# One Trainium2 core, mixer, cross-attention and routed experts: six PSUM banks and reordered evictions in the front, another order of the last eight weight chunks

## The reference

```python
hn = rmsnorm(h, g_mix); proj = hn @ w_in                  # 2048 columns: u | B | C | v
y_pool = pool_mixer(u, w_pool, pool_scale)                # trailing means over 2, 4, 8, 16 frames, 4 linear maps
y_conv = B * causal_conv3(C * v)
h = h + concat(y_pool, y_conv) @ w_out
h = h + mem_cross_attention(rmsnorm(h, g_xattn), rmsnorm(mem, g_mem), w_q, w_k, w_v, w_o)   # 4 heads of 256
xt = rmsnorm(h, g_moe); top 4 of 32 experts by xt @ w_router + b_router, gates = softmax(top 4)
gu = xt[tok] @ w_gate_up[e] + b_gate_up[e]                # 1024 -> 2048
act = (clip(gu_up, -7, 7) + 1) * (min(gu_gate, 7) * sigmoid(1.702 * min(gu_gate, 7)))
h[tok] += gate * (act @ w_down[e] + b_down[e])
out = rmsnorm(h, g_final)
```

## Time and profile before

| | |
|---|---|
| median of 3 runs | 1146.5 us (1143.35 to 1148.73) |
| profiled execution | 1145.61 us, its span 1143.9 us |
| front, to the last matmul of the logits | about 216 us |
| first chunk of the experts used | about 231 us |
| experts, 402.7 MB of weights | the rest |
| HBM read | 435.47 MB |
| granted TensorE clock, mean | 0.992 |

### The profile page before, as it was taken

How to read it: one execution, slowest core, us unless ns; L and a number is a source line. 1 busy time by engine, 2 the same in 40 slices (tenths; PEclk the granted TensorE clock), 3 DMA queues, 4 the chain that set the end, 5 groups by cost and what they waited for, 6 DMA issues and landing times.

```text
span 1143.9 us, 12842 instructions
## 1 busy us (share of the span) xinstructions
PE 1076.5 (94%) x5419; PEld 489.2 (43%) x5420; DVE 342.6 (30%) x573; ACT 197.7 (17%) x323; POOL 26.1 (2%) x53
## 2 busy tenths in 40 slices
PE   8979999999999999999999999999999989999995
PEld 7978997733333333333333333333332333333332
DVE  8555645312222222222222222222222212222223
ACT  6523544400000000000000110100000000000002
POOL 6200000000000000000000000000000000000000
PEclk9999999899999999999999999999999999999998
DMA  9964555789999999999999999999999999999993
GB/s 351 349 212 146 170 221 229 286 365 428 427 426 427 430 427 427 427 429 427 427 426 429 428 428 426 429 427 428 427 429 426 428 427 428 429 427 426 429 429 156
DMA packets 52007, 437.94 MB, mean 383 GB/s; under 512 B 5184, under 2 KB 23024, under 8 KB 27376
## 3 DMA queue, kind: packets, MB, share of 16 engines
q1 hardware_dynamic: 51856, 437.10, 92.0%
q10 hardware_dynamic: 96, 0.02, 0.0%
HBM read 435.47 MB, written 1.05 MB: 382 GB/s over the span
## 4 chain that ended last, share of the span: by engine, by line
PE 63%; DMA 25%; DVE 8%; ACT 2%; issue 1%; ACTq 0%; DVEq 0%
PE ps L734 26%; DMA slot<-in_w_gate_up 25%; PE ps L768 14%; PE ps L476 7%; PE ps L534 6%; PE ps L779 3%; PE ps L752 2%; DVE glu L1338 2%; DVE lin L1335 2%; DVE glu L1331 2%; DVE lin L1332 1%; ACT sig L824 1%; PE ps L499 1%; PE ps L723 1%; ACT w_hi L824 1%
## 5 line engine op out<-in xcount | busy, mean ns | idle before, releaser
L734 PE MATMUL ps<-slot,xT 128*64 128x512 f32 x2048 | 456.9, 595 | 17.2 <-DMA slot<-in_w_gate_up 16.4
L734 PEld LDWEIGHTS ps<-slot,xT 128*64 128x64 f32 x2048 | 142.0, 136 | 310.4 <-issue 266.1
L768 PE MATMUL ps<-slot,sig 128*64 128x512 f32 x1024 | 226.8, 595 | 8.0 <-ACT sig L824 8.0
L1344 DVE TENSOR_TENSOR h_rows<-ps,h_rows 128x1024 f32<-128x1024 f32 x64 | 75.4, 1219 | 368.3 <-PE ps L779 368.3
L768 PEld LDWEIGHTS ps<-slot,sig 128*64 128x64 f32 x1024 | 70.7, 137 | 143.6 <-issue 127.9
L995 ACT ACTIVATE sig<-glu 128x512 f32<-128x512 f32 x32 | 20.2, 632 | 546.3 <-DVE glu L1331 546.3
L1331 DVE TENSOR_SCALAR glu<-ps 128x512 f32<-128x512 f32 x32 | 22.1, 692 | 280.1 <-PE ps L734 280.1
L1093 DVE TENSOR_TENSOR w_lo<-ring,w_hi 128x1024 fp32r<-128x1024 f32 x56 | 68.2, 1225 | 74.7 <-ACT w_hi L824 74.6
L824 ACT ACTIVATE xg_sb<-ps 128x512 f32<-128x512 f32 x65 | 38.9, 598 | 245.3 <-PE ps L768 230.0
L824 ACT ACTIVATE w_hi<-ring 128x1024 fp32r<-128x1024 f32 x56 | 59.0, 1062 | 83.8 <-PE ps L476 52.3
L779 PE MATMUL ps<-xg_sb,g_sb 64*128 64x512 f32 x256 | 63.6, 615 | 0.7 <-ACT xg_sb L824 0.7
(11 more groups left out here) (190 smaller groups left out, 708.8 us busy)
## 6 DMA issues: line engine op xcount, KB each, us to landing
slot<-in_w_gate_up SPq DMA_DIRECT2D x128, 2048.0 KB, 36.4
slot<-in_w_down SPq DMA_DIRECT2D x64, 2048.0 KB, 37.5
ring<-in_w_in SPq DMA_DIRECT2D x8, 1024.0 KB, 13.9
ring<-in_w_v SPq DMA_DIRECT2D x4, 1024.0 KB, 10.6
ring<-in_w_out SPq DMA_DIRECT2D x4, 1024.0 KB, 12.1
ring<-in_w_k SPq DMA_DIRECT2D x4, 1024.0 KB, 5.7
ring<-in_w_q SPq DMA_DIRECT2D x4, 1024.0 KB, 5.2
ring<-in_w_o SPq DMA_DIRECT2D x4, 1024.0 KB, 4.8
```

What stands on the lines that cost most here:

```text
L734: mm = pe.matmul(ps[CAP * half:CAP * (half + 1), bank, :], lhsT, w[:, a * CHUNK + bank * D + half * HALF:a * CHUNK + bank * D + (half + 1) ...
L768: mm = pe.matmul(ps[CAP * half:CAP * (half + 1), bank_y, :], lhsT, w[:, r * D + half * HALF:r * D + (half + 1) * HALF], start=False, stop= ...
L1344: dve.tensor_tensor(h_rows[:, t, :].rearrange("p (a n) -> p a n", a=2), ps[:, b:b + 2, :], h_rows[:, t, :].rearrange("p (a n) -> p a n", a ...
```

## The change

1. Banks: `A_USES` is spread over banks 0 to 5 by a table. The first uses that follow a row product in banks 2 to 5 wait for that bank's eviction; the row products wait for the last small product of their bank.
2. Order on ACT and DVE: evictions go ahead of splits whose turn is not due, and `conv_in` is cut in two, the product with C (which frees the banks) and the three taps, later.
3. Start: the memory gain is loaded and transposed by itself; the other five rows are transposed after PE's third half of `w_v`, and ACT copies them ahead of the squares of `x`. The first 1 MB chunk is loaded as two halves. `frame_no` and its reciprocal shrink from 256 to 16 columns; POOL sets the others.
4. Routing: ACT's pass to `n_rows` goes; DVE multiplies `sel` by the frames' scale (`sel_rstd`), and PE gathers from `h_rows` itself. The sums go to a buffer of their own. Gate/up chunks hold other rows (16 KB of each 32 KB in place of 16 KB of each 64 KB), and the token transposes read `xg_sb` with a step of four.
5. End: chunks in the order expert 31 gate/up, expert 30 down, expert 31 down; expert 30's scatter stands between the two chunks of expert 31's down; the last chunk comes as four loads of 512 KB; `g_final` is asked for three chunks earlier. No gather for an expert 32.

```diff
-A_USES = ["u0", "u1", "C0", "v0", "d0", "C1", "v1", "pool0", "d1", "B0", "pool1", "B1", "k0", "k1", "k2", "k3",
-          "q0", "q1", "s0", "q2", "s1", "q3", "s2", "s3", "o0", "o1", "o2", "o3", "logits"]
+A_BANK = dict(u0=0, u1=1, C0=2, v0=3, d0=0, C1=4, v1=5, pool0=1, d1=0, B0=2, pool1=3, B1=0, k0=1, k1=0, k2=2, k3=3,
+              q0=4, q1=5, s0=0, q2=1, s1=2, q3=3, s2=4, s3=5, o0=0, o1=1, o2=0, o3=1, logits=0)
+A_USES = list(A_BANK)
+FIRST_AFTER_ROWS = {"C0": 0, "v0": 1, "C1": 2, "v1": 3, "k2": 0, "k3": 1, "q0": 2, "q1": 3}
...
+                if name in FIRST_AFTER_ROWS:
+                    pe.wait_ge(row_free if name[0] in "Cv" else h_added, FIRST_AFTER_ROWS[name] + 1)
...
-                    if k == 0 and n == 0 and bank_free is not None:
-                        pe.wait_ge(bank_free, r + 1)
+                    if k == 0 and n == 0 and last_use is not None:
+                        pe.wait_ge(a_free[bank_row[r]], a_uses(bank_row[r], last_use))
...
-            lo(16, 17, 18, 19)
-            conv_in(0)
-            lo(20, 21, 22, 23)
-            conv_in(1)
+            lo(16, 17, 18)
+            conv_product(0)
+            lo(19)
+            conv_taps(0)
+            lo(20, 21, 22)
+            conv_product(1)
+            lo(23)
             dve.wait_ge(bias_split, 2 * PARTS - 1)
             pool_out(0)
-            lo(24, 25)
+            lo(24)
+            conv_taps(1)
             gate_conv(0)
+            lo(25)
             pool_out(1)
...
-            largest(0), lo(48, 49)
-            scale_probs(0), largest(1), lo(50)
-            turned(0), lo(51), scale_probs(1)
-            largest(2), largest(3), scale_probs(2), scale_probs(3)
+            largest(0), lo(48), scale_probs(0), lo(49)
+            largest(1), turned(0), scale_probs(1), lo(50, 51)
+            largest(2), scale_probs(2), largest(3), scale_probs(3)
...
             hi(1, 2, 3)
+            t_out("vec", lambda bank, done: copy(vec[:, 0:N_ROWS], bank[:, 0:N_ROWS], done))
+            act_e.wait_ge(t_free[1], t_use("vec")[1])
             for c in range(TC):
                 act_e.wait_ge(x_in[c], 16)
                 square(1, c, h_rows, squares_out, squares)
...
+                dve.tensor_tensor(sel_rstd[:], sel[:], rstd, ALU.mult).then_inc(sel_rstd_ok, 1)
...
-                        mm = pe.matmul(ps[CAP * half:CAP * (half + 1), bank_xg, :], sel[:, t, :],
-                                       n_rows[:, t, half * HALF:(half + 1) * HALF], start=(t == 0), stop=(t == TC - 1),
+                        mm = pe.matmul(ps[CAP * half:CAP * (half + 1), bank_xg, :], sel_rstd[:, t, :],
+                                       h_rows[:, t, half * HALF:(half + 1) * HALF], start=(t == 0), stop=(t == TC - 1),
...
+            gate_up(E - 1, (E - 1) % 2, ring_chunk(E - 1))
+            pe.wait_ge(aT_ok, E - 1)
+            turn_gates(E - 1, (E - 1) % 2)
+            down(E - 2, ring_chunk(E - 2))
+            pe.wait_ge(y_ok, E - 1)
+            bias_down((E - 1) % 2)
+            turn_act(E - 1)
+            down(E - 1, ring_chunk(E - 1), last=True)
+            pe.wait_ge(sc_added, (E - 1) * TC - 1)
+            scatter(E - 1, gates=g_last)
...
+            for r in range(4):
+                sp.dma_start(slots[SLOT_ORDER[(TOTAL - 1) % RING]][:, D * r:D * (r + 1)], last[:, r, :]).then_inc(tail_in[r], 16)
```

More of the change, by code:

```diff
@@ L458, in a_begin @@
             def a_begin(name):
-                n = a_use(name)
-                if n >= 2:
-                    pe.wait_ge(a_free[n % 2], n // 2)
-                return ps[:, n % 2, :]
+                bank = A_BANK[name]
+                before = a_uses(bank, name) - 1
+                if before:
+                    pe.wait_ge(a_free[bank], before)
+                if name in FIRST_AFTER_ROWS:
+                    pe.wait_ge(row_free if name[0] in "Cv" else h_added, FIRST_AFTER_ROWS[name] + 1)
+                return ps[:, bank, :]
             def split_half(j):
@@ L543, in _ @@
             keep_clock(9)
-            pe.wait_ge(vec_in, 16 * 6)
-            bank, done = t_begin("vec")
-            pe.transpose(bank[:, 0:N_ROWS], vec_rows[:], ident[0:N_ROWS, 0:N_ROWS]).then_inc(done, 1)
+            pe.wait_ge(mem_gain_in, 16)
+            bank, done = t_begin("vecm")
+            pe.transpose(bank[:, 0:KC], mem_gain_rows[:], ident[0:KC, 0:KC]).then_inc(done, 1)
             for c in range(TC):
@@ L556, in _ @@
                 project_rows("w_v", k, mn_hi, mn_lo)
+                if k == 2:
+                    pe.wait_ge(vec_in, 16 * 5)
+                    bank, done = t_begin("vec")
+                    pe.transpose(bank[:, 0:N_ROWS], vec_rows[:], ident[0:N_ROWS, 0:N_ROWS]).then_inc(done, 1)
                 if k in (4, 6):
@@ L771, in down, with scatter @@
                     mm.then_inc(chunks_used, 1)
-            def scatter(s):
+                    if last and h == 0:
+                        scatter(s - 1, second=0)
+            def scatter(s, second=2, gates=g_sb):
                 pe.wait_ge(y_ok, s + 1)
@@ L778, in scatter @@
                         rws = slice(CAP * half, CAP * (half + 1))
-                        mm = pe.matmul(ps[:, (4 if t == 0 else 2) + half, :], g_sb[rws, t * P:(t + 1) * P],
+                        mm = pe.matmul(ps[:, (4 if t == 0 else second) + half, :], gates[rws, t * P:(t + 1) * P],
                                        y_sb[rws, :], start=True, stop=True, skip_group_check=True)
                     mm.then_inc(sc_full, 1)
-            pe.wait_ge(scaled, 1 + TC)
             gather(0)
@@ L816, in again, with dummy @@
                 scatter(s)
-            more_rounds(pe, most, again)
+            def dummy():
+                gather(E)
+                turn_tokens(E)
+            more_rounds(pe, most, again, dummy)
         @block.scalar
@@ L883, in _ @@
             fetch_table(ACT.Sqrt)
-            t_out("vec", lambda bank, done: copy(vec[:], bank[:, 0:N_ROWS], done))
+            t_out("vecm", lambda bank, done: copy(vec[:, ROW_MEM:ROW_MEM + KC], bank[:, 0:KC], done))
             act_e.wait_ge(t_free[1], 1)
@@ L978, in _ @@
             fetch_table(ACT.Exp)
-            act_e.wait_ge(rstd_ok, 1)
-            for c in range(TC):
-                act_e.activation(n_rows[:, c, :].rearrange("t (k p) -> t k p", p=P),
-                                 h_rows[:, c, :].rearrange("t (p k) -> t k p", p=P), ACT.Copy,
-                                 scale=stat[:, 3, 2, c:c + 1]).then_inc(scaled, 1)
             act_e.wait_ge(route_neg, 1)
@@ L1355, in _, with prepare, prepare_and_activate @@
             most = load_most(dve)
-            def prepare_and_activate(s, par):
-                select(s + 1, s + 1, par)
-                weigh(s + 1, s + 1, par)
-                activate(s)
+            def prepare(s, par):
+                select(s, s, par)
+                normalise_selected(s)
+                weigh(s, s, par)
+            def prepare_and_activate(s, par, used):
+                prepare(s + 1, par)
+                activate(s, used)
                 tokens_out(s + 1, par)
-            prepare_and_activate(0, 1)
-            add_back(0)
-            prepare_and_activate(1, 0)
-            with dve.Fori(1, E // 2) as turn:
+            prepare_and_activate(0, 1, GATE_UP)
+            add_back(0, before=h_rows)
+            prepare_and_activate(1, 0, PER_EXPERT + GATE_UP)
+            with dve.Fori(1, E // 2 - 1) as turn:
                 e0 = turn * 2
```

247 lines of the change are left out of this document (148 added, 99 removed).

## The result

| | before | after |
|---|---|---|
| median | 1145.1 us (4 runs, 1143.35 to 1148.73) | 1129.21 us (4 runs, 1128.75 to 1130.88) |
| profiled execution, its span | 1145.61, 1143.9 | 1129.19, 1127.5 |
| mean granted clock | 0.992 | 0.998 |

The ratio is 0.986, interval 0.9831 to 0.9888: 15.9 us faster, outside the range (1132 to 1143) on the fast side. The gain forecast was 8.9 by the profiled executions and came out as 16.4. In a later comparison the changed kernel took 1129.67 (4 runs) and the kernel before 1144.66 (17 runs), 15.0 apart: ratio 0.9859, 0.984 to 0.9878.

The account below looks back on a forecast made before the run. Weight loads at 427 GB/s set the pace, so the end stands a fixed distance behind the first issue after the full ring. From 1145.6: +1.4 - 8.8 - 2.1 + 0.5 + 0.1 = -8.9, 1136.7; median 1137.6, range 1132 to 1143.

Parts of the forecast that it names:

- The mixer: Mixer: PE's four idle times (C1, d1, B0, B1), together 9.16, go; w_out then waits 0.4: -8.8 us.
- The same work stands there now: Routing: the clock at 0.54 of full from 216 to 226, after 32 narrow logits matmuls, was expected to stay.
- its bound of -2: Routing: if the clock fell elsewhere, the gather's 3.68 would halve or first gate/up matmuls take twice as long: -2 to +3.
- The attention: Attention: two waits of 1.62 for scaled probabilities go, shorter ones appear at heads 2 and 3: -2.1 us, bounds -3.2 and 0.
- The start: Start up to u0: PE comes 2.06 earlier, but ACT's wait for the other five rows delays x's tiles: +1.4 us.
- The routing's new step: Routing: scaled selection between sel and gather +0.4, stepped token transposes +0.1: together +0.5 us, bounds 0.3 and 0.8.
- The loads: Weight loads: the gate/up chunks' new row step leaves the rate at 427 GB/s: 0 us.
- The end: End: 15.2 us from third-last landing against 15.0, +0.1 to +0.2; early order and four parts give nothing.
- DVE as the bound: Rival, mixer: evictions ahead of splits make lo late, only half of 9.16 comes back: 1142 us; chance 0.14.
- slower loads: Rival, expert loads: new gate/up row step slows them, at 3% 1156 us; chance 0.08, 0.06 of it slower by over 0.5%.
- hidden work at the end: Rival, end: scatter and copy hide beside waits for data, 3.5 us more gain: 1134 us; chance 0.08.
- The start pays in full: Rival: u0 not held by ACT's wait, start -2.1, and attention nearly in full, -3: 1133 us; chance 0.14.

Follow-up runs that it names:

- the banks alone: Kernel before with only the six-bank table (part 1), evictions in their old places, start, routing and end of before: 1130.29 us, ratio 0.9866.
- The matmuls among the logits: Kernel before with one 128x128 matmul into an unused bank added behind each of the first three groups of the logits: 1144.22 us, ratio 0.9988.

## Why the prediction was wrong

Between the profiled executions 7.5 us are missing from the forecast gain (16.4 for 8.9): 4.0 in the routing, 1.4 in the mixer, 1.3 in the start, 0.5 in the attention and 0.3 at the end.

**The mixer** was right in mechanism and short by 1.4: all four waits went, what came next was the wait for w_out's bank (0.4 predicted, 0.29 measured, and it falls behind w_out's start), but the term "together 9.16" counted idle time alone. The stretch shrank by 10.18; the other 1.02 are 0.17 to 0.35 at each of the four restarts, which the row of the idle time doesn't hold. A row that follows without a stall begins while the one before it is still under way: in the changed kernel C1's first matmuls start 0.14 behind the start of a row of 0.38 us.

**The step that failed most**, by the profiled executions, is the clock. "The same work stands there now" took the 0.54 of the routing for a property of the code. It was one of the executions: 3.4 us of the 7.5 that are missing between the profiled executions. The prediction did name a gain, if the fall came elsewhere, but its bound of -2 was sized by the gather alone, and 3.4 lies outside it.

For the medians, by which the time came out below the range, the reason is another. The routing's long fall is in one of six profiles with the routing code of before, so hardly in most executions, and yet the median fell by 15.0. The terms measured are 10.2 in the mixer, 2.1 in the attention and 2.5 for the clock falls behind the stalls: 14.8. They come from different comparisons, with intervals of about 2 us to either side, so that they meet so closely is in part luck; for the banks alone the same sum is 1.7 short of the medians. The term of 2.5 stood in no step of the prediction; its profile had none to show. So by the medians the step that failed is the pricing of the stalls: their idle time alone, with nothing for restart and clock, where the runs show 10.2 and 2.5 for the 8.8 of the sum.

**The attention** was sized right, 2.1. The profiles' 2.57 hold 0.5 of the clock.

**The start** was +1.4 and came out as 0: u0 at 36.8 to 37.2 in five profiles of the changed start, at 36.3 to 38.7 in seven of the old one. The mechanism is there on both sides: PE came to its first product 2.42 earlier, ACT's wait gave that back, and moving the copy wins it, -2.6. The queues that the prediction followed were too slow, by 1.4 at u0: PE turned the rows at 18.15, not at 19.03, and ACT went on at 18.68, not at 19.7. The old start's spread makes the 0 a rough figure; its wait for the last small load alone was 2.04 to 3.43 us long.

**The routing's new step** was +0.5 and is -0.1. "The scaled frames on ACT were done before the selection" holds only for the slow clock; at full clock they were 0.80 late, and that wait went when 0.60 for the scaled selection came.

**The loads** were right: 0. **The end** was right too: 15.27 for 15.2, and no price for four loads. The price that the prediction worked out from the Trainium skill, DMA: Bandwidth & Descriptors, 2 us for each part and the last bytes 6 us later, didn't come: the last bytes came 4.95 behind the chunk before, those of the single load 4.9. (That fit is for loads issued from GpSimd; these come from SP.) PE came to the last chunk at 1111.68, 1.8 behind its last part.

**The rivals.** DVE as the bound, slower loads and hidden work at the end were all refuted by rows. "The start pays in full" names 1133, nearest to the result, but its start of -2.1 isn't there in this version, and its attention of -3 was 2.1.

**Open:** what decides in which execution the clock falls, and why the profiled execution of before had the long fall in its routing, which five other profiles with the same routing code don't show. In the routing PE had done 32 narrow matmuls of the logits before the clock fell, in that profile and in the changed kernel's second one; the last idle time before them was 0.60 us, and it stands in the profiles without the fall as well. The matmuls among the logits didn't settle it.

## What to carry to other kernels

An idle time of PE of about 2 us ahead of dense work was worth more here than its row: 0.25 for the restart, and in some executions 1.5 more at half clock; fill it with products that compute nothing if it can't be removed, and look at the profile of several executions before a low clock is booked as the code's. A wait may stand on a queue only as early as its result is needed: a small copy for later work, put ahead of the squares, cost as much as its removal from PE's path had won.

## What the runs showed of the hardware

Removing work made the kernel slower: without eight matmuls that compute nothing, together 2.0 us long, it took 2.2 us more. Filling stalls with them made the kernel before 2.5 us faster though no wait ended earlier. And an idle time need not be long for it: falls followed idle times of 1.79, 1.81, 1.92, 2.14, 2.28 and 3.10 us, while in other executions the same 2.14 and 3.09 were followed by full clock. At the end of a stream of 2 MB loads a chunk that came as four loads of 512 KB landed 4.95 us behind the chunk before it, one that came as a single load 4.9.
